# An experts' stage: gate and up products of 64 tokens in 512-column pieces into one half of the partitions, in place of 256-column pieces into both halves

## The reference

```python
def expert_block(args):
    xblk, e = args
    hid = jax.nn.silu(xblk @ w_gate[e]) * (xblk @ w_up[e])
    return hid @ w_down[e]
```

## Time and profile before

| | |
|---|---|
| median of 3 runs | 2440.95 us (2440.74 to 2443.25) |
| the profiled execution | 2440.75 us, its span 2439.5 us |
| TensorE busy | 2238.5 us, 92% of the span |
| VectorE, ScalarE, GpSimd busy | 937.8, 709.5, 589.0 us |
| memory read | 562.14 MB |
| first and last record of the experts' matmuls | 885.99 and 1807.05 us from the span's start |

### The profile page before, as it was taken

One profiled execution on the slowest core, in us unless ns is written; L12 is line 12 of the kernel. 1 busy time (PEld: TensorE's weight loads), 2 busy tenths in 40 slices (PEclk: granted clock), 3 DMA queues, 4 the chain that ended last, 5 costly groups with the idle time before them and its releaser, 6 DMA issues.

```text
span 2439.5 us, 32498 instructions
## 1 busy us (share of the span) xinstructions
PE 2238.5 (92%) x13082; PEld 1651.6 (68%) x13082; DVE 937.8 (38%) x1874; ACT 709.5 (29%) x1386; POOL 589.0 (24%) x682
## 2 busy tenths in 40 slices
PE   7999999999999989998888788788879999999999
PEld 5777888888888555554444444444447857888887
DVE  5677677777322431110000000000027575542441
ACT  4545556565321110000000000000024485431330
POOL 4443576676000011111111111111114170000000
PEclk9999999999999999999999999999999999999999
DMA  6322233343445479999999999999984202223220
GB/s 188 97 81 71 91 126 117 104 156 123 162 172 215 186 313 428 428 428 429 429 428 429 429 429 428 429 428 429 429 330 145 90 33 70 74 99 104 104 103 35
DMA packets 148938, 572.82 MB, mean 235 GB/s; under 512 B 14940, under 2 KB 75896, under 8 KB 124080
## 3 DMA queue, kind: packets, MB, share of 16 engines
q1 hardware_dynamic: 127440, 533.63, 54.8%
q0 software_dynamic: 15632, 26.43, 3.3%
q10 hardware_dynamic: 5712, 10.62, 1.5%
HBM read 562.14 MB, written 29.43 MB: 242 GB/s over the span
## 4 chain that ended last, share of the span: by engine, by line
PE 66%; DMA 19%; DVE 6%; issue 3%; POOL 3%; SPq 2%; ACT 2%; another core or an unknown queue 1%; ACTq 0%; DVEq 0%; POOLq 0%
PE ps L720 14%; PE ps L722 13%; PE ps L721 13%; PE ps L1130 10%; DMA ringy<-in_w_expert_up 6%; PE ps L1160 5%; DMA ring<-in_w_expert_up 4%; DMA ringx<-in_w_expert_up 4%; PE ps L713 3%; PE ps L963 2%; DMA ringx<-in_w_expert_gate 2%; DMA ring<-in_w_expert_gate 2%; SPq L651 2%; PE ps L825 1%
## 5 line engine op out<-in xcount | busy, mean ns | idle before, releaser
L2456 DVE TENSOR_TENSOR sg<-ps,sg 128x256 f32<-128x256 f32 x64 | 27.2, 425 | 816.4 <-PE ps L1130 816.4
L720 PE MATMUL ps<-hTh,hb 128*128 128x512 f32 x576 | 237.4, 412 | 3.0 <-DVE ringr L1985 3.0
L722 PE MATMUL ps<-hTh,ringr 128*128 128x512 f32 x576 | 226.1, 392 | 0.0
L721 PE MATMUL ps<-hTl,hb 128*128 128x512 f32 x576 | 225.3, 391 | 0.0
L1772 ACT COPY ys<-ps 128x512 f32<-128x512 f32 x64 | 37.4, 585 | 618.3 <-PE ps L1160 618.3
L1130 PE MATMUL ps<-ringx,gxT 128*64 128x256 f32 x1536 | 186.4, 394 | 31.4 <-DMA ringx<-in_w_expert_up 20.9
L1130 PE MATMUL ps<-ringy,gxT 128*64 128x256 f32 x1504 | 181.6, 392 | 33.0 <-DMA ringy<-in_w_expert_up 20.7
L1130 PEld LDWEIGHTS ps<-ringx,gxT 128*64 128x64 f32 x1536 | 126.4, 136 | 98.1 <-issue 54.6
L1130 PEld LDWEIGHTS ps<-ringy,gxT 128*64 128x64 f32 x1504 | 123.6, 135 | 98.1 <-issue 58.7
L1985 DVE TENSOR_TENSOR ringr<-ring,hb 128x1024 fp32r<-128x1024 f32 x112 | 147.9, 1322 | 91.3 <-ACT hb L1479 90.5
L2881 POOL DMA_INDIRECT gx<-h2d,rows x64 | 65.4, 1021 | 484.2 <-PE ps L713 476.8
(11 more groups left out here) (449 smaller groups left out, 4640.8 us busy)
## 6 DMA issues: line engine op xcount, KB each, us to landing
ringx<-in_w_expert_up SPq DMA_DIRECT2D x25, 2048.0 KB, 50.7
ringy<-in_w_expert_gate SPq DMA_DIRECT2D x24, 2048.0 KB, 50.2
ringx<-in_w_expert_gate SPq DMA_DIRECT2D x23, 2048.0 KB, 49.2
ringx<-in_w_expert_down SPq DMA_DIRECT2D x23, 2048.0 KB, 49.3
ringy<-in_w_expert_up SPq DMA_DIRECT2D x23, 2048.0 KB, 49.3
ringy<-in_w_expert_down SPq DMA_DIRECT2D x22, 2048.0 KB, 50.5
ring<-in_w_expert_down SPq DMA_DIRECT2D x18, 2048.0 KB
ring<-in_w_expert_gate SPq DMA_DIRECT2D x17, 2048.0 KB
```

Source lines behind the costliest of these rows:

```text
L720: pe.matmul(o, lh, rh, start=start and n == 0, stop=False)
L721: pe.matmul(o, lh, rl, start=False, stop=False)
L722: m = pe.matmul(o, ll, rh, start=False, stop=stop and n == len(ks_) - 1)
```

## The change

The product of an expert is made in one piece of 512 columns in place of two of 256, into the lower 64 partitions for even e and the upper 64 for odd e. So one product is 8 calls in place of 16. `sg` becomes one tile [128, 512], whose halves belong to even and odd experts. Silu and the multiplication work on 64 partitions x 512 elements in place of 128 x 256. `hidden_turned` makes four transposes of 64 partitions x 128 elements (every fourth element of a row) in place of two of 128 x 128 (every second), and `down` finds its slices in `hidT` in another order. `turned`, the calls of `down`, the DMAs, the slots, the semaphores and all the waits stay as they are.

```diff
-    sgs = sbs("sg", 2, [128, 256], WE)
+    sg2 = sb("sg", [128, 512], F32, WE)
+    sgs = [sg2[0:64, :], sg2[64:128, :]]
...
+    def half(t, e):
+        return t[e % 2 * 64:e % 2 * 64 + 64, :]
+
...
-                w4 = w3.rearrange("p k (n j) -> p k n j", j=4)
                 pe.wait_ge(semaphore, value)
                 for k in range(8):
-                    for c in range(2):
-                        m = pe.matmul(b[c * 64:c * 64 + 64, 0:256].rearrange("p (n j) -> p n j", j=2),
-                                      gxTs[e % 2][:, k % 4, k // 4 * 64:k // 4 * 64 + 64],
-                                      w4[:, k, :, 2 * c:2 * c + 2], start=k == 0, stop=k == 7)
+                    m = pe.matmul(half(b, e), gxTs[e % 2][:, k % 4, k // 4 * 64:k // 4 * 64 + 64],
+                                  w3[:, k, :], start=k == 0, stop=k == 7)
...
-            hid = sgs[e % 2][:, :].rearrange("p (n j) -> p n j", j=2)
-            for j in range(2):
-                m = pe.transpose(b[:, j * 128:j * 128 + 128], hid[:, :, j], ident)
+            hid = sgs[e % 2].rearrange("p (n j) -> p n j", j=4)
+            for j in range(4):
+                m = pe.transpose(b[:, j * 64:j * 64 + 64], hid[:, :, j], half(ident, e)[:, e % 2 * 64:e % 2 * 64 + 64])
...
-                    m = pe.matmul(b[c * 64:c * 64 + 64, :], hidTs[e % 2][:, k % 2, k // 2 * 64:k // 2 * 64 + 64],
+                    m = pe.matmul(b[c * 64:c * 64 + 64, :], hidTs[e % 2][:, k // 2, k % 2 * 64:k % 2 * 64 + 64],
                                   w3[:, k, c * 512:c * 512 + 512], start=k == 0, stop=k == 3)
...
-                a.activation(sgs[e % 2][:, :], banks[2 + e % 2][:, 0:256], ACT.Silu).then_inc(s["e_sg"], 1)
+                a.activation(sgs[e % 2], half(banks[2 + e % 2], e), ACT.Silu).then_inc(s["e_sg"], 1)
...
-                v.tensor_tensor(sgs[e % 2][:, :], banks[4 + e % 2][:, 0:256], sgs[e % 2][:, :], MUL).then_inc(s["e_hd"], 1)
+                v.tensor_tensor(sgs[e % 2], half(banks[4 + e % 2], e), sgs[e % 2], MUL).then_inc(s["e_hd"], 1)
```

## The result

The changed kernel takes 2754.66 us (median of 4 runs, 2753.72 to 2756.14) against 2441.13 us before: slower by the ratio 1.1284, 95% interval 1.127 to 1.1297. The forecast was 2761 us, range 2740 to 2825. The profiled execution took 2755.06 us, with a span of 2753.8 us.

What follows compares the result with a forecast made beforehand. TensorE was taken to pace 15 rounds and transfers the rest; afterwards TensorE throughout. Rounds of 12.65 + 6.46 + 0.27 = 19.38 us, 61 of them plus both ends, put the stage 320.7 us later: 2761 us, range 2740 to 2825.

Steps and rivals of the forecast that it cites:

- What bounds the stage: Experts' stage: TensorE paces 15 rounds of 12.65 us, then transfers pace 46 of 15.00, leaving TensorE about 2.35 us spare.
- A record alone and in a pair: Products: 0.429 us per 512-column MATMUL; different halves overlap, one call's two records do not, so a product takes 6.86 us.
- Gate and up, + 6.46 us a round: Gate and up products: each goes from 3.63 to 6.86 us, 3.23 more each, 6.46 together.
- The upper bound, 0.454 us for a record: Gate and up: twice what up shows for 256 columns, adding 0.8 us a round.
- The multiplication, + 0.27 us: VectorE's 64 x 512 multiplication, on the path to `down`: 0.69 us in place of 0.42; lower bound 0.
- The start of the stage, and the second part: First product at 885.99 us as before, 33.12 us to the first `down`; the part behind the experts' stage unchanged.
- The transposes, silu, the transfers at nothing: Four transposes, 0.58 us silu and 14.7 us transfers stay covered, costing nothing; transposes' upper bound about 0.4 us a round.
- A lone half at twice the rate: Rival for the products: one call's two records overlap, a product takes 3.4 us, time stays 2441 us; 4 in 100.
- The weight load in the open: Rival for the products: each of 32 MATMULs waits for its load, 2.8 us a round, 2940 us; 3 in 100.
- The clock: Sign that the forecast is wrong: a granted clock under 1 within the experts' stage; no size or chance given.

Runs made afterwards that it cites:

- the paired kernel: Changed kernel with the gate product in the other half than up, the calls of both taking turns slice by slice: 2445.78 us, 1.0018 of the kernel before.

## Why the prediction was right

**What bounds the stage.** Right: TensorE for the first rounds, the transfers afterwards, 2.35 us to spare. Every second expert in one piece passes it (16.0 us, 2547), every fourth (14.3 us) does not, apart from what the ends of the stage cost.

**A record alone and in a pair.** Right. Calls for the two halves overlap and the records of one call don't; the paired kernel undoes the loss and the one-piece kernels show 0.429 us for each record. The reason given for why alternating by expert does not help, that the products are no neighbours, was right in effect. The rule behind it was not complete: three records may lie between. `turned`, `hidden_turned` and `down` are 24 records.

**Gate and up, + 6.46 us a round.** Measured: 6.86 and 6.96 in place of 3.63 and 3.76, + 6.43. (The sum took 3.63 for both.) The upper bound, 0.454 us for a record, belonged to the skipping operand and did not apply.

**The multiplication, + 0.27 us.** The term that was mis-sized. I took the difference of two durations. What lengthens the way to `down` is the time to the next operation's start: + 0.21 us in the upper half and + 0.10 in the lower. The earlier trace rows had the second of these: the operation behind the 128 x 256 multiplication starts 929.83 - 929.32 = 0.51 us after it, and the one behind the 128 x 512 scaling 930.44 - 929.83 = 0.61 us. From the start of the transposes to `down` it is 2.02 and 1.89 us, for 1.81. The mean, + 0.145, is 0.125 us short of my term, 61 x 0.125 = 7.6 us, nearly all of the 8.0 us between the forecast's stage end (2127.7) and the measured one (2119.7).

**The start of the stage, and the second part.** Two errors that cancel in part. The way from the first product to the first `down` was forecast at 33.12 us and took 918.66 - 885.01 = 33.65, with a first gate product of 894.28 - 885.01 = 9.27 us in place of the 5.28 of the earlier trace rows: the granted clock was 0.88 over 885 to 905 us here, and 0.91 over 886 to 905.6 us before. The first product of this execution happened to start 0.98 us earlier than the one before. The second part was taken as unchanged and took 2753.8 - 2119.7 = 634.1 us for 2439.5 - 1807.05 = 632.4, so that of the 8.0 us 6.3 are left between 2761.4 and the profiled 2755.06. The granted clock over its first 200 us was 0.97 for 0.98 before; more was not looked for.

**The transposes, silu, the transfers at nothing.** Right: 0.11 us of the transposes' cover is left in the lower half's rounds and 0.23 in the upper's, silu takes 0.59 us within a product of 6.9, and no product waits for weights.

**The rivals.** A lone half at twice the rate: refuted, no step under 0.429 us within one half in the changed kernel. The weight load in the open: refuted, since 0.429 us is also the step of the full array and twice the loads cost 0.08 us a round. Its price was low besides: 0.086 us counts loads that overlap once, and one load lasts 0.136 us on average in the kernel before. The clock: 1.00 in every round from the first `down` on; it was below 1 at the stage's start, as in the kernel before.

## What to carry to other kernels

An fp32 matmul whose weights fill 64 columns costs TensorE as much as one that fills the array (0.429 us a record of 512 columns); what makes it cheap is a second one for the other half within a few records of the stream. Before splitting or joining pieces, write down for each half how many columns are streamed and which calls stand next to each other. When operations follow each other on one engine, add the distances between their starts, not their lengths. And the cover that an engine has to spare is not a mean over the rounds alone: it was smaller at the ends of this stage, and a test that needs room must not take it from a buffer on the last chain.

## What the runs showed of the hardware that I had not expected

- TensorE's records for a free half started up to three records ahead of their place: four records of 0.43 us overlapped at the border of two products in different halves, blocks of four records in turn overlapped in full, and with blocks of eight 32 records took 20 steps, so that 12 pairs of the 16 ran together.
- A moving operand that takes two fp32 elements of every four cost 5% of a product (3.63 against 3.45 us for as many columns side by side).
- The operation behind a 64 x 512 VectorE multiplication started 0.61 us after it when it worked in the lower 64 partitions, before it had ended, and 0.72 us when in the upper ones, behind its end. What makes the difference no run here shows.
